# Self attention in a long fused kernel: one head per step against two heads per step on the halves of the matmul array

## The reference

```python
def dilated_mixture(q, k, v):
    B, S = q.shape[:2]
    slopes = alibi_slopes(ATTN_HEADS)
    outs, lses = [], []
    for gi, (window, dilation) in enumerate(DIL_GROUPS):
        hs = slice(gi * HEADS_PER_GROUP, (gi + 1) * HEADS_PER_GROUP)
        o, l = dilated_attention(q[:, :, hs], k[:, :, hs], v[:, :, hs], window, dilation, slopes[hs])
        outs.append(o)
        lses.append(l)
    wts = jax.nn.softmax(jnp.stack(lses, axis=0), axis=0)
    y = jnp.sum(wts[..., None] * jnp.stack(outs, axis=0), axis=0)
    return y.reshape(B, S, ATTN_OUT_DIM)
```

## Time and profile before

| | us |
|---|---|
| median of 3 runs | 3574.42 (3573.76 to 3574.74) |
| the profiled execution: its own time | 3573.03 |
| its span in the trace | 3571.2 |
| PE busy | 3412.6 (96% of the span) |
| DVE busy | 1767.0 (49%) |
| ACT busy | 1182.6 (33%) |
| POOL busy | 482.9 (14%) |
| granted PE clock, mean over the span | 0.986 |

### The profile page before, as it was taken

How to read it: one execution, slowest core, us unless ns; L and a number is a source line. 1 busy time by engine, 2 the same in 40 slices (tenths; PEclk the granted TensorE clock), 3 DMA queues, 4 the chain that set the end, 5 groups by cost and what they waited for, 6 DMA issues and landing times. The chain is left out here.

```text
span 3571.2 us, 53321 instructions
## 1 busy us (share of the span) xinstructions
PE 3412.6 (96%) x22308; PEld 2787.1 (78%) x22308; DVE 1767.0 (49%) x1984; ACT 1182.6 (33%) x1472; POOL 482.9 (14%) x436
## 2 busy tenths in 40 slices
PE   7999999999999999999999999999998778999998
PEld 5578888888888888887578887887776776778887
DVE  7655243454344653436554344564686444555242
ACT  3633122432222232222632134233663442342122
POOL 1111011020010020111111012000141111111011
PEclk9999999999999999999999999999999999999999
DMA  3232233222223222333123223342221113313332
GB/s 127 62 99 95 94 99 102 83 95 94 94 95 105 94 95 96 95 104 105 55 92 105 94 94 107 106 136 89 92 88 64 39 45 120 108 59 99 102 94 71
DMA packets 314091, 329.64 MB, mean 92 GB/s; under 512 B 22834, under 2 KB 305461, under 8 KB 313397
## 3 DMA queue, kind: packets, MB, share of 16 engines
q1 hardware_dynamic: 307141, 303.39, 26.6%
q0 software_dynamic: 4464, 19.40, 1.6%
q10 hardware_dynamic: 2304, 4.20, 0.3%
HBM read 312.28 MB, written 14.68 MB: 92 GB/s over the span
## 5 line engine op out<-in xcount | busy, mean ns | idle before, releaser
L481 PE MATMUL ps<-xh,wh 128*128 128x512 f32 x2360 | 936.0, 397 | 25.7 <-DVE wl L422 22.3
L481 PE MATMUL ps<-xl,wh 128*128 128x512 f32 x2360 | 923.2, 391 | 0.0
L481 PE MATMUL ps<-xh,wl 128*128 128x512 f32 x2360 | 923.1, 391 | 0.0
L422 DVE TENSOR_TENSOR wl<-raw,wh 128x2048 fp32r<-128x2048 f32 (+2 forms) x287 | 641.7, 2236 | 464.4 <-ACT wh L417 463.8
L417 ACT ACTIVATE wh<-raw 128x2048 fp32r<-128x2048 f32 (+2 forms) x287 | 527.2, 1837 | 708.1 <-PE ps L481 675.9
L481 PEld LDWEIGHTS ps<-xh,wh 128*128 128x128 f32 x2360 | 446.4, 189 | 134.1 <-issue 37.8
L481 PEld LDWEIGHTS ps<-xl,wh 128*128 128x128 f32 x2360 | 446.4, 189 | 96.9 <-issue 5.0
L481 PEld LDWEIGHTS ps<-xh,wl 128*128 128x128 f32 x2360 | 445.7, 189 | 94.0
L481 PE MATMUL ps<-hh,wh 128*128 128x512 f32 x1280 | 498.5, 389 | 1.2 <-DVE wl L422 1.0
L481 PE MATMUL ps<-hl,wh 128*128 128x512 f32 x1280 | 498.0, 389 | 0.0
L481 PE MATMUL ps<-hh,wl 128*128 128x512 f32 x1280 | 498.0, 389 | 0.0
(11 more groups left out here) (417 smaller groups left out, 3555.7 us busy)
## 6 DMA issues: line engine op xcount, KB each, us to landing
raw<-in_mlp_w SPq DMA_DIRECT2D x128, 1024.0 KB, 5.1
raw<-in_ffn_w SPq DMA_DIRECT2D x32, 1024.0 KB, 5.4
raw<-in_w_in SPq DMA_DIRECT2D x31, 1024.0 KB, 5.3
raw<-in_a_w_in SPq DMA_DIRECT2D x20, 1024.0 KB, 5.2
raw<-in_c_w_in SPq DMA_DIRECT2D x12, 1024.0 KB, 5.0
raw<-in_a_w_out SPq DMA_DIRECT2D x16, 640.0 KB, 4.0
raw<-in_b_w_in SPq DMA_DIRECT2D x8, 1024.0 KB, 5.4
raw<-in_xa_wkv SPq DMA_DIRECT2D x8, 1024.0 KB, 5.2
```

Source lines behind the costliest of these rows:

```text
L422: nc.vector.tensor_tensor(wl[:, p.slot(su), 0:n], raw[:, p.slot(su), 0:n], wh[:, p.slot(su), 0:n], ALU.subtract).then_inc(lower, 1)
L481: last = nc.tensor.matmul(banks[mt][:, 0:st.n], wt[at_, slot, k, mt * P:mt * P + P], ops[oi][at_, kk, 0:st.n], start=k == 0 and su == 0 an ...
```

## The change

Two heads of the same query block are taken at once, so that there are 8 pairs instead of 16 combinations. The heads of a pair lie in partitions 0 to 63 and 64 to 127 of qT and kT: their scores go to the two row halves of the array and to different banks (`attn_scores`), matmul by matmul in turn. Their products with the values go to the two column halves, matmul by matmul in turn, and land in partitions 0 to 63 and 64 to 127 of one bank (`attn_values`). The transposes of both heads stand in one run of twelve (`attn_turns`).

The slots keep their places, but what stands in them is spread: pair k has its scores, the bias, the maximum and the exponentials in slot 2k; the division on DVE in slot 2k+1; transposes and ACT's copies in slot 2k+3; values and the output copy in slot 2k+5. So an even slot holds scores, an odd one values (of one pair) and transposes (of the next). The last values are in slot 19. `early` is gone from v, memk and memv; in gates it holds the middle slot's part of DVE. The tile `sc` has two places of two heads, `pt` moves to another address and overlaps `w2a2`, and so the DMAs of `w2a2` wait for the last values and are issued behind the weights of lora.

```diff
@@ -175,16 +175,16 @@
-    sc = at("sc", 41, [P, 3, 768])
-    pt = at("pt", 50, [P, 2, 6, P])
+    sc = at("sc", 41, [P, 2, 2, 768])
+    pt = at("pt", 84, [P, 2, 6, P])
-    den = at("den", 56.5, [P, 6])
+    den = at("den", 56.5, [P, 8])
-    stat = at("stat", 56.25, [P, 6])
+    stat = at("stat", 56.25, [P, 8])
...
-    combos = [(h, i) for h in range(4) for i in range(4)]
+    pairs = [(hp, i) for hp in range(2) for i in range(4)]
     slopes = [2.0 ** (-8.0 * (k + 1) / 12) for k in range(12)]
...
+    NPAIR = len(pairs)
+    LOHI = (slice(0, 64), slice(64, P))
     def after_group(st, c):
         return {"v": c - 1, "memk": 2 + c, "memv": 6 + c, "gates": 11 + 2 * c}.get(st.name, -1)
+    def attn_scores(pe, k):
+        hp, i = pairs[k]
+        own = slice(i * P, i * P + P)
+        if k == 0:
+            pe.wait_ge(evac, (stages["k"].g0 + 3) * 2 + 4)
+            pe.wait_ge(s("mem_split"), ND)
+        else:
+            pe.wait_ge(s("at_scored"), k)
+        if k >= 2:
+            pe.wait_ge(s("at_pt"), k - 1)
+        if k >= 3:
+            pe.wait_ge(s("at_copied"), k - 2)
+        for e in range(2):
+            nc.tensor.matmul(ps[4 + e][:], qT[LOHI[e], hp, own], kT[LOHI[e], hp], start=True, stop=True)
+        for g in (1, 2):
+            for e in range(2):
+                last = nc.tensor.matmul(ps[6 + e][:, g * P - P:g * P], qT[LOHI[e], 2 * g + hp, own], kT[LOHI[e], 2 * g + hp, own],
+                                        start=True, stop=True)
+        last.then_inc(s("at_scores"), 1)
+    def attn_values(pe, n):
+        hp, i = pairs[n]
+        if n == 0:
+            pe.wait_ge(evac, (stages["v"].g0 + 3) * 2 + 4)
+        else:
+            pe.wait_ge(s("at_copied"), n)
+        pe.wait_ge(s("at_scored"), min(n + 3, NPAIR))
+        pe.wait_ge(s("at_pt"), n + 1)
+        for b in range(6):
+            g, kc = (0, b) if b < 4 else (b - 3, i)
+            for e in range(2):
+                v0 = (4 * g + 2 * hp + e) * 64
+                last = nc.tensor.matmul(ps[7][LOHI[e], 256:384], vt[:, kc, v0:v0 + 64], pt[:, e, b], start=b == 0, stop=b == 5)
+        last.then_inc(s("at_pv"), 1)
+    def attn_turns(pe, j):
+        pe.wait_ge(s("at_scored"), min(j + 2, NPAIR))
+        pe.wait_ge(s("at_probs"), j + 1)
+        if j:
+            pe.wait_ge(s("at_pt"), j)
+        for e in range(2):
+            for b in range(6):
+                n_ = 6 * e + b
+                last = nc.tensor.transpose(ps[4 + n_ // 4][:, n_ % 4 * P:n_ % 4 * P + P], sc[:, j % 2, e, b * P:b * P + P], ident[:])
+        last.then_inc(s("at_turned"), 1)
     def pe_attn_slot(pe, k):
...
+        if k >= 0 and k % 2 == 0 and k // 2 < NPAIR:
+            attn_scores(pe, k // 2)
+        if k % 2 and 0 <= (k - 5) // 2 < NPAIR:
+            attn_values(pe, (k - 5) // 2)
+        if k % 2 and 0 <= (k - 3) // 2 < NPAIR:
+            attn_turns(pe, (k - 3) // 2)
+    def dve_attn_slot(dve, p):
+        if p >= 0 and p % 2 == 0 and p // 2 < NPAIR:
+            k = p // 2
+            hp, i = pairs[k]
+            r = k % 2
             dve.wait_ge(s("at_scores"), k + 1)
...
+            if k >= 2:
+                dve.wait_ge(s("at_turned"), k - 1)
+            for e in range(2):
+                h = 2 * hp + e
+                nc.vector.scalar_tensor_tensor(out=sc[:, r, e, 0:512], in0=dist[:, 3 - i:7 - i].rearrange("p a n -> p (a n)"),
+                                               scalar=-8.0 * slopes[h], in1=ps[4 + e][:], op0=ALU.mult, op1=ALU.add)
+                for g in (1, 2):
+                    ins = nc.vector.scalar_tensor_tensor(out=sc[:, r, e, 384 + g * P:512 + g * P], in0=dist[:, 6 + g],
+                                                         scalar=-8.0 * slopes[4 * g + h], in1=ps[6 + e][:, g * P - P:g * P],
+                                                         op0=ALU.mult, op1=ALU.add)
             ins.then_inc(s("at_scored"), 1)
             dve.wait_ge(s("at_scored"), k + 1)
...
+            link(nc.vector.tensor_reduce(stat[:, 4 * r:4 * r + 2], sc[:, r], AX.X, ALU.max))
+            nc.vector.tensor_scalar(stat[:, 4 * r + 2:4 * r + 4], stat[:, 4 * r:4 * r + 2], -0.125, None, ALU.mult).then_inc(s("at_max"), 1)
+        if p % 2 and 0 <= (p - 5) // 2 < NPAIR:
+            n = (p - 5) // 2
+            hp, i = pairs[n]
+            dve.wait_ge(s("at_pv"), n + 1)
+            nc.vector.tensor_copy(by4(ya[:, hp])[:, :, i], ps[7][:, 256:384]).then_inc(s("at_copied"), 1)
+        if p % 2 and 0 <= (p - 1) // 2 < NPAIR:
+            k = (p - 1) // 2
+            r = k % 2
+            dve.wait_ge(s("at_exp"), 2 * k + 2)
+            link(nc.vector.reciprocal(den[:, 4 * r + 2:4 * r + 4], den[:, 4 * r:4 * r + 2]))
+            for e in range(2):
+                ins = nc.vector.tensor_scalar(sc[:, r, e], sc[:, r, e], den[:, 4 * r + 2 + e:4 * r + 3 + e], None, ALU.mult)
+            ins.then_inc(s("at_probs"), 1)
+    def act_attn_slot(act, p):
+        if p >= 0 and p % 2 == 0 and p // 2 < NPAIR:
+            k = p // 2
+            r = k % 2
             act.wait_ge(s("at_max"), k + 1)
...
+            for e in range(2):
+                act.activation(sc[:, r, e], sc[:, r, e], ACT.Exp, scale=0.125, bias=stat[:, 4 * r + 2 + e:4 * r + 3 + e],
+                               accum_out=den[:, 4 * r + e:4 * r + e + 1]).then_inc(s("at_exp"), 1)
+        if p % 2 and 0 <= (p - 3) // 2 < NPAIR:
+            j = (p - 3) // 2
+            act.wait_ge(s("at_turned"), j + 1)
+            if j:
+                act.wait_ge(s("at_pv"), j)
+            flat_pt = pt[:].rearrange("p e b n -> p (e b n)")
+            for b in range(3):
+                ins = act.activation(flat_pt[:, b * 512:b * 512 + 512], ps[4 + b][:], ACT.Copy)
+            ins.then_inc(s("at_pt"), 1)
+    def dve_before_gates(p):
+        dve_attn_slot(nc.vector, 10 + 2 * p.c)
...
-        if name == "memv":
-            sp.wait_ge(s("mem_turned"), ND // 2)
+        if name == "lora":
+            sp.wait_ge(s("at_pv"), NPAIR)
             sp.dma_start(w2a2[0:64], a["w2_2"][0]).then_inc(s("lora_landed"), 16)
             sp.dma_start(w2a2[64:P], a["a2_2"][0]).then_inc(s("lora_landed"), 16)
...
-        dve_stage(dve, G["v"], custom=dve_tok, early=dve_before(G["v"]))
-        dve_stage(dve, G["memk"], custom=dve_kv, early=dve_before(G["memk"]))
-        dve_stage(dve, G["memv"], custom=dve_kv, early=dve_before(G["memv"]))
-        dve_stage(dve, G["gates"], custom=dve_gates, early=dve_before(G["gates"]))
+        dve_stage(dve, G["v"], custom=dve_tok)
+        dve_stage(dve, G["memk"], custom=dve_kv)
+        dve_stage(dve, G["memv"], custom=dve_kv)
+        dve_stage(dve, G["gates"], custom=dve_gates, early=dve_before_gates)
```

More of the change, by code:

```diff
@@ L1178, in dve_tok @@
                 ins.then_inc(evac, 1)
-        dve_attn_scores(nc.vector, after_group(G["v"], p.c))
+        dve_attn_slot(nc.vector, after_group(G["v"], p.c))
     def pe_rscol(pe):
@@ L1192, in dve_rscol @@
         dve.wait_ge(s("mem_normed"), 1)
-    combos = [(h, i) for h in range(4) for i in range(4)]
+    pairs = [(hp, i) for hp in range(2) for i in range(4)]
     slopes = [2.0 ** (-8.0 * (k + 1) / 12) for k in range(12)]
-    NCOMBO = len(combos)
+    NPAIR = len(pairs)
+    LOHI = (slice(0, 64), slice(64, P))
     def after_group(st, c):
         return {"v": c - 1, "memk": 2 + c, "memv": 6 + c, "gates": 11 + 2 * c}.get(st.name, -1)
-    def pe_attn_slot(pe, k):
[L1207 to L1238, removed]
-            o = ps[7][64 * (h % 2):64 * (h % 2) + 64, 256 + n % 2 * P:384 + n % 2 * P]
-            for b in range(6):
-                g, kc = (0, b) if b < 4 else (b - 3, i)
-                last = nc.tensor.matmul(o, vt[:, kc, (4 * g + h) * 64:(4 * g + h) * 64 + 64], pt[:, n % 2, b],
-                                        start=b == 0, stop=b == 5)
-            last.then_inc(s("at_pv"), 1)
@@ L1246, in dve_attn_scores @@
-    def dve_attn_scores(dve, k):
-        if 0 <= k < NCOMBO:
-            h, i = combos[k]
-            r = k % 3
-            dve.wait_ge(s("at_scores"), k + 1)
-            if k >= 3:
-                dve.wait_ge(s("at_turned"), k - 2)
-            x0 = (3 - i) * P
-            nc.vector.scalar_tensor_tensor(out=sc[:, r, 0:512], in0=dist[:, 3 - i:7 - i].rearrange("p a n -> p (a n)"),
-                                           scalar=-8.0 * slopes[h], in1=ps[4][:], op0=ALU.mult, op1=ALU.add)
-            for g in (1, 2):
-                ins = nc.vector.scalar_tensor_tensor(out=sc[:, r, 384 + g * P:512 + g * P], in0=dist[:, 6 + g],
-                                                     scalar=-8.0 * slopes[4 * g + h], in1=ps[5][:, g * P - P:g * P],
-                                                     op0=ALU.mult, op1=ALU.add)
+    def attn_scores(pe, k):
[17 more added lines that the diff above has]
+        last.then_inc(s("at_scores"), 1)
@@ L1281, in act_attn_slot @@
-    def act_attn_slot(act, k):
-        if 0 <= k < NCOMBO:
-            r = k % 3
```

(12 more changed lines are left out.)

27 lines of the change are left out of this document (2 added, 25 removed).

## The result

The changed kernel takes 3546.21 us (median of 4 runs, 3539.55 to 3547.74), beside 3574.58 for the kernel before (3573.76 to 3574.79): 0.9918 of its time, with a 95% interval of 0.9905 to 0.9930. The forecast was 3552.7, a gain of 21.7; the measured gain is 28.4. The direction and both overlaps held; the term for the clock did not.

A forecast was written before the change was run, and what follows sets the result against it. PE, busy in 96% of the span, was taken to bound the kernel. Gains of 14.8 us in gates and 6.9 before slot 10 made 21.7, from 3574.4 to 3552.7 us; range 3546 to 3563, 8 times in 10.

The forecast's parts named there:

- both overlaps: PE: two heads' scores on row halves and products on column halves cost what one head did, 1.50 and 1.46 us.
- the term for the clock: Falls of PE's granted clock behind waits at slots 3 to 9: three at 1.7 us each, 5.1 us lost.
- Scores of a pair: PE, even slots: two heads' scores on two row halves take 1.50 us; 2.8 us without overlap.
- products: PE, odd slots: two heads' value products on two column halves take 1.46 us; bound 2.75 us.
- the maximum: DVE, even slots: the maximum over two heads takes 1.75 us, between 0.95 and 1.90.
- the chain from scores to weights: In v, memk, memv: from an even slot's start until PE can start the group after next, 12.0 us.
- waits 1.7 and 3.2: PE waits for weights in memk and memv: 1.7 us, and 3.2 us behind slot 3, which has no values.
- two groups: Memk and memv: two groups take 17.9 us, where PE's own work would allow 16.4.
- gates 79.0: From slot 10 to DVE's last gates evacuation: 79.0 us instead of 93.8, a gain of 14.8.
- Twelve transposes: PE, odd slots: a pair's twelve transposes take 1.4 us, bounds 1.3 and 1.6.
- Rival 1: The clock does not fall behind PE's waits, or once only: up to 5.1 us less, 3548 us; chance 14%.
- The bounds without overlap: PE: if the array halves did not overlap, a pair's scores would take 2.8 us, its products' matmul part doubled 2.75.

The follow-up runs named there:

- third execution: The changed kernel unedited, run again a second time: 3543.02 us, ratio 0.9907, attention stretch 168.77 us.
- rows in series: Changed kernel with the scores of one head, then of the other, instead of in turn: 3554.55 us, ratio 0.9948.
- the three comparisons: The changed kernel timed three times against the kernel before: 3546.21, 3548.78 and 3543.02 us, ratios 0.9918, 0.9919 and 0.9907.
- the series runs: Changed kernel with one head after the other: scores only 3554.55 us, value products only 3548.39 us, both 3561.57 us.
- half of the maximum once more: Changed kernel with one more maximum over one of the two heads in each even slot: one run, 3555.56 us.

## Why the forecast was off, step by step

**Right, within 0.5 us.** Scores of a pair 1.50 (1.50), products 1.46 (1.46), the maximum 1.75 (1.75), the chain from scores to weights 12.0 (11.94), waits 1.7 and 3.2 (1.51 and 3.12), two groups 17.9 (17.85), gates 79.0 (78.64), no wait in gates, division, copies and the w2a2 loads at no cost (the two loads are issued at 2460, 36 us before rkv's first pair). Twelve transposes took 1.28 us where 1.4 was forecast.

On the columns the rule of the Trainium skill ("TensorE: Matmul & The Clock Gate", Part 3, that a weight load overlaps matmuls in flight only where its row group differs) does not hold in this trace: both halves share all 128 rows, and 24 records took 1.53 us in turn and 2.45 one head after the other. The rule speaks of weight loads; that the products of a pair would then cost near 2.75 us was the forecast's own step from it.

**The step that failed** is "I count a fall at slot 3 for certain and at two of the three slots 5, 7 and 9: 3x1.7 = 5.1". There was one, at slot 3, for 1.50 us, so this term was too large by 3.6. I had taken two rows for a rule. That there was exactly one is luck in part: the same program had none in its third execution, and then 168.77 us. The runs give in its place, for PE's waits for L422 at slots 3 to 9 in the kernels with such waits:

| wait, us | clock fell behind it |
|---|---|
| 0.57 to 0.59 | 0 of 6 |
| 1.49 to 1.51 | 0 of 18 |
| 2.51 | 2 of 3 |
| 3.10 to 3.12 | 5 of 8 |
| 3.30 to 4.90 | 5 of 5 |

A fall is read from the granted clock, or, in some runs at 1.5 us and less, from two groups that take no more than their 17.85 us (18.82 with rows in series). Yet in before the clock fell behind 1.04 us, a wait that stood inside the slot, between the scores and the transposes. And ahead of rkv's first group the wait was 3.43 or 3.44 us in all fourteen traces, while the clock fell behind it in twelve. So the length is not all, and what else counts is open. The cost is no constant either: one fall took between 1.44 and 2.85 us, where the forecast put 1.7.

**What adds up.** The gain of the profiled executions is 3573.03-3547.74 = 25.3: attention stretch 25.8, lora's fall that didn't come 1.5, 1.6 ahead of slot 0 and less 3.6 in rkv, chunks and the rest; the last three lie in code that the change left alone. Of the stretch's 25.8 the forecast had 21.7; the falls are 3.6 of the difference, gates 0.4, the rest roundings. The medians differ by 28.4: the profiled execution of after is 1.5 us above its median and that of before 1.6 below its own. Those 3 us are in no trace, and the three comparisons (gains of 0.82%, 0.81% and 0.93%, each uncertain by 0.13 to 0.2%, that is by 5 to 7 us) say that the medians move by that much.

**What the range left out.** It took in the bounds of the attention's costs alone. The stages behind differ by up to 8.7 us between executions of one program, more than the 6.7 between forecast and low end, and the four timed runs of after by 8.2. A few us more at either end were due on that ground alone. Rival 1 with its 3548 came nearest to what happened; its case holds in the trace.

**The bounds without overlap** (2.8 and 2.75 us for a pair) were not reached by the series runs, 2.46 and 2.39. That does not refute them: there four records of the first head still ran beside the second. With these the starts give some 2.9 and 2.8.

## What to carry to other kernels

Read in the trace whether a control run switches off what it is meant to. One head after the other looked like no overlap and left the halves together for some 0.44 us a block. Taken at its word it gives the halves 12 of 27 us; with what was left they have some 18, an estimate, and falls of the clock, larger blocks and shorter waits have the rest. Look also at what stands in ACT's or DVE's queue ahead of the next weights: putting the weights first was worth another 8 to 10 us and took no work away. Judge a change of this size by the stretch that it touches, which repeats to 0.03 us with the same falls of the clock, and not by one total.

## What the runs showed of the chip that was not expected

- Two column halves over the same 128 rows overlap fully, 24 fp32 records of 128 columns in 1.53 us; one half after the other, 2.45.
- When a second head's matmuls follow the first's on the other half, they don't wait for its end: the first of them started beside the fourth-last record of the first head, on row halves (2340.14 and 2340.13) and on column halves (both 2369.41). What sets the number four is open.
- The same wait (3.12 us) in the same program was followed by a granted clock of 0.57 in two executions and of 1.00 in a third. One fall costs between 1.44 us (2.51 us wait at slot 7, half of the maximum once more) and 2.85 us (lora's stretch of 17.08 against 14.23) here.
